# A Fourier mixer branch on one Trainium2 core: positions before channels, on sums and differences of token halves

## The chip, the cores and the metric

One core of one Trainium2 chip runs the whole program. The metric is device microseconds of one execution. All data is float32; matrix products run on pairs of numbers, a rounded high part (fp32r) and the remainder, called `hi` and `lo` below.

## The reference

An encoder layer for 512 tokens (SEQ) of 1024 features. The part that matters here is the mixer between the two feed-forward halves:

```
h = RMSNorm(x)
[q | k | v | f | g_a | g_b] = h @ w_in           # 512 | 128 | 128 | 512 | 1024 | 1024 columns
y_a = WindowGQA(q, k, v) @ w_branch_a
y_b = Re(FFT2 over (position, channel of a group)(f)) @ w_branch_b     # 4 groups of 128 channels
x = x + (sigmoid(g_a) * y_a + sigmoid(g_b) * y_b) @ w_out
```

With scale s = 1/sqrt(512*128), the Fourier branch of one group with the 512x128 matrix f is s*(C f c - S f d), where C and S are the 512x512 tables of cosines and sines over positions and c and d those of size 128 over channels.

## The kernel before

Every product `w*x` is three matmuls: w_hi with x_hi, w_hi with x_lo, w_lo with x_hi. One operand is loaded into the array (LDWEIGHTS, 128x128) and the other streams through it (up to 512 columns). A *granule* is one output tile of 128 features by 512 tokens: eight 128-row tiles of a weight matrix, each loaded in turn, while the tokens' columns stream, 24 matmuls of 512 columns. Weights come by DMA (issued by SP) into one of four slots of `raw`; ACT rounds a slot to `w_hi` (`split_hi`, L577), DVE subtracts to get `w_lo` (`split_lo`, L948), both four granules ahead, and both only when TensorE has used the slot's previous content (`w_used`).

All engines run fixed lists written out by hand, each engine in its own program order, tied by semaphores. In the mixer, one list (`MIXER`, L162) is read by ACT, DVE and TensorE (the loops at L819, L1238 and L1682); its first steps are

```
f 0; f 1; f 2; f 3; channels 0; k; v; positions 0; channels 1; q 0; positions 1; channels 2; q 1;
positions 2; channels 3; q 2; turn_v; positions 3; q 3; scores 0 0;
...
```

A step `f`, `k`, `v` or `q` is one granule on TensorE; then DVE reads the result out of PSUM and multiplies by the norm's factor of each token (`rstd`, made once during f 1 from sums of squares), ACT rounds it and DVE forms the remainder. In step `k` ACT writes four half-height tiles `kp_hi` and DVE four `kp_lo`. `channels g` multiplies, for each of the four blocks of 128 tokens, the block of f (loaded in the array) with the 256 columns of c and d: 12 matmuls of 256 columns, whose results, `ab`, have tokens on the partitions. ACT and DVE split them to `ab_hi` and `ab_lo`. `positions g` multiplies them with the position tables for outputs 0 to 257: two sums (even with C, odd with S) over four token blocks, 24 matmuls of 258 columns. ACT copies the even part to `even_t`; DVE adds and subtracts the odd part to obtain the 512 outputs in `y_t` (L1293, L1295), which ACT and DVE split to `fy_hi` and `fy_lo`. Each of these, and the two per-token sums at L1514 and L1524, waits for its inputs and for the PSUM bank that it overwrites to have been read.

Of the kernel before, what the change touches and what calls it, by code (L numbers as in the profile page):

```python
# [66 lines left out]
O_K = O_F + N_FGROUPS  # L67
# [9 lines left out]
B_SUM, B_RSTD = 4, 5  # L77
B_CH, B_POS = 4, 6
# [24 lines left out]
NPOS = SEQ // 2 + 2  # L103
CH_AT = TB * 2 * NPOS
TABLE = CH_AT + 2 * FG_DIM

# [23 lines left out]
def shape_constants():  # L130

    s, k = np.arange(SEQ)[:, None], np.arange(NPOS)[None, :]
    turn = 2 * np.pi * ((s * k) % SEQ) / SEQ
    scale = 1.0 / np.sqrt(SEQ * FG_DIM)
    pos = np.concatenate([np.cos(turn) * scale, -np.sin(turn) * scale], axis=1)
    pos = pos.reshape(TB, P, 2 * NPOS).transpose(1, 0, 2).reshape(P, CH_AT)
    c = np.arange(FG_DIM)
    turn = 2 * np.pi * ((c[:, None] * c[None, :]) % FG_DIM) / FG_DIM
    tables = np.concatenate([pos, np.cos(turn), np.sin(turn)], axis=1).astype(np.float32)
    onehot = np.zeros((N_BUCKETS, NREL + 1), np.float32)  # L140
    onehot[t5_buckets(), NREL - 1 - np.arange(NREL)] = 1.0
    return {"tables": tables, "onehot": onehot}


def window(nb):
# [17 lines left out]
    f 0; f 1; f 2; f 3; channels 0; k; v; positions 0; channels 1; q 0; positions 1; channels 2; q 1;  # L163
    positions 2; channels 3; q 2; turn_v; positions 3; q 3;
# [60 lines left out]
def build(nc, io):  # L225
# [10 lines left out]
    with ExitStack() as ctx:  # L236
# [13 lines left out]
        even_t, _, _ = place("even_t", [P, NPOS], F32)  # L250
# [39 lines left out]
        s_t = [s_a, s_b]  # L290
        y_t, _, _ = place("y_t", [P, SEQ], F32)
# [37 lines left out]
        ab_hi, ab_at = reuse("ab_hi", [P, TB, 2 * FG_DIM], F32R)  # L329
        ab_lo, _ = reuse("ab_lo", [P, TB, 2 * FG_DIM], F32R)  # L330
# [7 lines left out]
        tab_lo, _ = reuse("tab_lo", [P, TABLE], F32R)  # L338
        tab_raw, _, _ = place("tab_raw", [P, TABLE], F32, bias_at)

        pt_hi, pt_at, pt_size = place("pt_hi", [P, 2, GQ * BLK], F32R, ab_at)
        pt_lo, _, _ = place("pt_lo", [P, 2, GQ * BLK], F32R, ab_at + pt_size)
# [30 lines left out]
        pt_hi_ready, o_hi_ready, ab_hi_ready = sem("pt_hi_ready"), sem("o_hi_ready"), sem("ab_hi_ready")  # L373
        even_copied, y_hi_ready, m_hi_ready = sem("even_copied"), sem("y_hi_ready"), sem("m_hi_ready")
# [9 lines left out]
        pt_lo_ready, o_lo_ready, ab_lo_ready = sem("pt_lo_ready"), sem("o_lo_ready"), sem("ab_lo_ready")  # L384
# [9 lines left out]
        ab_done, even_done, odd_done, y_turned = sem("ab_done"), sem("even_done"), sem("odd_done"), sem("y_turned")  # L394
# [33 lines left out]
        def x_bank(m):  # L428

            return 8 - X_BANKS + m % X_BANKS  # L430

# [20 lines left out]
        def _(sp):  # L452
# [42 lines left out]
            for r in range(2):  # L495
# [77 lines left out]
        def _(act):  # L573
# [225 lines left out]
            for r in range(2):  # L799
# [19 lines left out]
                for step in steps:  # L819
                    kind = step[0]  # L820
                    if kind == "f":
                        grp = step[1]
                        split_hi(G_F + grp + SLOTS)
                        act.wait_ge(out_read, O_F + grp + 1)
                        copy(fy_hi[:, grp, :], gate_t[grp % 2][:, :]).then_inc(proj_hi_ready, 1)
# [24 lines left out]
                    elif kind == "turn_v":  # L850
                        act.wait_ge(v_turned, 1)
                        copy(v_hi[:, :, :], banks[B_CH][:, :]).then_inc(v_hi_ready, 1)
                    elif kind == "channels":
                        grp = step[1]
                        for i in range(2):
                            act.wait_ge(ab_done, 2 * grp + i + 1)
                            copy(ab_hi[:, 2 * i:2 * i + 2, :], banks[B_CH + i][:, :]).then_inc(ab_hi_ready, 1)
                    elif kind == "positions":
                        grp = step[1]
                        act.wait_ge(even_done, grp + 1)  # L860
                        if grp:
                            act.wait_ge(y_ready, 2 * grp)
                        copy(even_t[:, :], banks[B_POS][:, 0:NPOS]).then_inc(even_copied, 1)
                        act.wait_ge(y_ready, 2 * grp + 2)
                        copy(fy_hi[:, grp, :], y_t[:, :]).then_inc(y_hi_ready, 1)
# [79 lines left out]
        def _(dve):  # L945
# [35 lines left out]
            def factors(n):  # L981

                dve.wait_ge(rstd_done, n + 1)
                vec.tensor_copy(rstd[:, :], banks[B_RSTD][:, :]).then_inc(rstd_ready, 1)
                dve.wait_ge(rstd_ready, n + 1)

            def mean(n, blocks=(0, TB), nth=0):
                t0, t1 = blocks
                dve.wait_ge(sum_done, n + 1 + nth)
                vec.tensor_scalar(var[:, t0:t1], banks[B_SUM][:, 2 * t0:2 * t1:2], 1.0 / D_MODEL, EPS, ALU.mult,  # L990
# [233 lines left out]
            for r in range(2):  # L1224
# [13 lines left out]
                for step in steps:  # L1238
                    kind = step[0]
                    if kind == "f":  # L1240
                        grp = step[1]
                        split_lo(G_F + grp + SLOTS)
                        if grp == 0:
                            norm_factors(NORM_MIX)
                        dve.wait_ge(w_used, G_F + grp + 1)
                        vec.tensor_tensor(gate_t[grp % 2][:, :], banks[(O_F + grp) % BANKS][:, :], rstd[:, :],
                                          ALU.mult).then_inc(out_read, 1)
                        dve.wait_ge(proj_hi_ready, grp + 1)
                        lo(fy_lo[:, grp, :], gate_t[grp % 2][:, :], fy_hi[:, grp, :]).then_inc(proj_lo_ready, 1)
# [3 lines left out]
                    elif kind == "k":  # L1253
# [3 lines left out]
                        dve.wait_ge(proj_hi_ready, N_FGROUPS + 1)  # L1257
# [8 lines left out]
                    elif kind == "q":  # L1266
# [6 lines left out]
                        dve.wait_ge(proj_hi_ready, N_FGROUPS + 2 + c)  # L1273
# [3 lines left out]
                    elif kind == "turn_v":  # L1277
                        dve.wait_ge(v_hi_ready, 1)
                        lo(v_lo[:, :, :], banks[B_CH][:, :].rearrange("p (t d) -> p t d", t=TB),
                           v_hi[:, :, :]).then_inc(v_lo_ready, 1)  # L1280
                    elif kind == "channels":
                        grp = step[1]
                        for i in range(2):
                            dve.wait_ge(ab_hi_ready, 2 * grp + i + 1)
                            lo(ab_lo[:, 2 * i:2 * i + 2, :],
                               banks[B_CH + i][:, :].rearrange("p (t d) -> p t d", t=2),
                               ab_hi[:, 2 * i:2 * i + 2, :]).then_inc(ab_lo_ready, 1)
                    elif kind == "positions":

                        grp, h = step[1], SEQ // 2  # L1290
                        dve.wait_ge(odd_done, grp + 1)
                        dve.wait_ge(even_copied, grp + 1)
                        vec.tensor_tensor(y_t[:, 0:h + 1], even_t[:, 0:h + 1], banks[B_POS + 1][:, 0:h + 1],  # L1293
                                          ALU.add).then_inc(y_ready, 1)
                        vec.tensor_tensor(y_t[:, SEQ - 1:h:-1], even_t[:, 1:h], banks[B_POS + 1][:, 1:h],  # L1295
                                          ALU.subtract).then_inc(y_ready, 1)
                        dve.wait_ge(y_hi_ready, grp + 1)
                        lo(fy_lo[:, grp, :], y_t[:, :], fy_hi[:, grp, :]).then_inc(y_lo_ready, 1)
                    elif kind == "scores":
# [157 lines left out]
        def _(pe):  # L1457
# [56 lines left out]
            def sum_squares(n):  # L1514
# [4 lines left out]
                for t in range(TB):  # L1519
                    mm = nc.tensor.matmul(banks[B_SUM][:, 2 * t:2 * t + 2], ssum[:, t * P:(t + 1) * P], ones[:, 0:2],  # L1520
# [3 lines left out]
            def spread_factors(n):  # L1524

                pe.wait_ge(diag_ready, n + 1)
                nc.tensor.matmul(banks[B_RSTD][:, :], ones[:, :], gb_t[:, :], start=True, stop=True).then_inc(rstd_done, 1)
# [137 lines left out]
            for r in range(2):  # L1665
# [15 lines left out]

                for step in steps:  # L1682
# [199 lines left out]
```

## Time and profile before

| | us |
|---|---|
| median of 3 runs | 1013.51 (1012.17 to 1013.98) |
| the profiled execution | 1014.11 |
| its span in the trace | 1012.3 |
| TensorE matmuls busy in it | 997.7 |
| VectorE (DVE) busy | 679.0 |
| ScalarE (ACT) busy | 440.1 |

The span is the time from the first to the last recorded instruction; 1.8 us of the profiled execution lie outside it. Matmuls overlap, so the start of one to the start of the next tells more of their cost than the duration that the trace gives each. The mixer's first `f` matmul starts 365.87 us into the span and `channels 0` at 389.49 us; the first `scores` matmul starts at 439.87 us.

### The profile page before, as it was taken

Reading aid. Unit: us, or ns where it says so; the run is one execution under the profiler, and the core shown is the slowest. Engines: PE = TensorE matmul, PEld = TensorE weight load, DVE = VectorE, ACT = ScalarE, POOL = GpSimd, SP = SyncE. Lnnn points to the kernel's source line nnn. Section 1 sums busy time; section 2 is a strip of 40 time slices with the busy share of each in tenths; the row PEclk is TensorE's granted clock in tenths of the full one; section 3 lists DMA queues with packets and bytes.
Section 4 is the critical chain, followed back from the end, with each engine's and each line's share of the span. In section 5 each row is a group of like instructions: output and inputs, shape, how many; then the busy total and the mean of one; then the engine's idle time right before and its main releaser. Section 6 shows DMA issues by size and latency. Waiting matters only on the chain. (4 is left out here: it accounts for less than half of the span.)

```text
span 1012.3 us, 16276 instructions
## 1 busy us (share of the span) xinstructions
PE 997.7 (99%) x5872; PEld 885.7 (87%) x5872; DVE 679.0 (67%) x924; ACT 440.1 (43%) x656; POOL 198.1 (20%) x113
## 2 busy tenths in 40 slices
PE   8999999999999999999999999999999999999997
PEld 7789999999788888888888888888999999978887
DVE  5778999999534346667765555458899999943332
ACT  5344444446322325346664334334445454633322
POOL 2452333340011110000000001324234333001101
PEclk9999999999999999999999999999999999999999
DMA  6423334323433364212213343322333332333222
GB/s 210 132 66 94 116 92 120 87 83 96 124 96 90 115 171 125 63 42 62 63 42 89 98 124 104 104 84 72 96 108 100 110 97 83 89 117 96 88 68 84
DMA packets 191816, 98.81 MB, mean 98 GB/s; under 512 B 13384, under 2 KB 190616, under 8 KB 191648
## 3 DMA queue, kind: packets, MB, share of 16 engines
q1 hardware_dynamic: 190560, 95.50, 32.3%
q10 hardware_dynamic: 1216, 2.78, 0.8%
q8 instruction: 25, 0.41, 0.2%
q14 instruction: 15, 0.12, 0.0%
HBM read 96.15 MB, written 2.11 MB: 97 GB/s over the span
## 5 line engine op out<-in xcount | busy, mean ns | idle before, releaser
L575 ACT ACTIVATE w_hi<-raw 128x1024 fp32r<-128x1024 f32 (+2 forms) x202 | 181.5, 902 | 231.6 <-PE bank L1496 155.2
L953 DVE TENSOR_TENSOR w_lo<-raw,w_hi 128x1024 fp32r<-128x1024 f32 (+2 forms) x138 | 150.0, 1089 | 145.7 <-ACT w_hi L575 144.2
L1595 PE MATMUL bank<-t_lo,w_hi 128*128 128x256 f32 x896 | 224.7, 283 | 0.0
L1593 PE MATMUL bank<-t_hi,w_hi 128*128 128x256 f32 x896 | 224.6, 283 | 0.0
L1595 PEld LDWEIGHTS bank<-t_lo,w_hi 128*128 128x128 f32 x896 | 172.0, 192 | 0.2
L1593 PEld LDWEIGHTS bank<-t_hi,w_hi 128*128 128x128 f32 x896 | 172.0, 192 | 0.2
L1430 POOL TENSOR_TENSOR ssum<-ssum,sq 128x512 f32<-128x512 f32 x27 | 41.4, 1533 | 535.2 <-ACT sq L612 534.4
L1599 PE MATMUL bank<-t_hi,w_lo 128*128 128x256 f32 x896 | 144.0, 283 | 0.0
L1484 PE MATMUL bank<-a_hi,w_hi 128*128 128x512 f32 (+1 forms) x374 | 140.6, 380 | 1.7 <-ACT a_hi L575 1.7
L1485 PE MATMUL bank<-a_lo,w_hi 128*128 128x512 f32 (+1 forms) x374 | 139.4, 377 | 0.0
L1599 PEld LDWEIGHTS bank<-t_hi,w_lo 128*128 128x128 f32 x896 | 123.6, 192 | 0.0
L1121 DVE TENSOR_TENSOR w_lo<-raw,w_hi 128x1024 fp32r<-128x1024 f32 x64 | 90.9, 1420 | 9.3 <-ACT w_hi L575 9.3
L575 ACT ACTIVATE w_hi<-raw_b 128x1024 fp32r<-128x1024 f32 x64 | 60.8, 949 | 80.0 <-POOL raw_b L1450 40.4
L1121 DVE TENSOR_TENSOR w_lo<-raw_b,w_hi 128x1024 fp32r<-128x1024 f32 x64 | 92.8, 1449 | 3.8 <-ACT w_hi L575 3.7
L1496 PE MATMUL bank<-a_hi,w_lo 128*128 128x512 f32 (+1 forms) x374 | 91.1, 377 | 0.0
L1484 PEld LDWEIGHTS bank<-a_hi,w_hi 128*128 128x128 f32 x374 | 70.3, 188 | 15.4 <-ACT a_hi L575 2.5
L1484 PE MATMUL bank<-h_hi,w_hi 128*128 128x512 f32 x208 | 81.9, 394 | 0.3 <-DVE ga_t L1270 0.3
L1485 PEld LDWEIGHTS bank<-a_lo,w_hi 128*128 128x128 f32 x374 | 70.4, 188 | 12.6
L1485 PE MATMUL bank<-h_lo,w_hi 128*128 128x512 f32 x208 | 81.1, 390 | 0.0
L1496 PEld LDWEIGHTS bank<-a_hi,w_lo 128*128 128x128 f32 x374 | 67.8, 188 | 12.9
L1484 PE MATMUL bank<-hf_hi,w_hi 128*128 128x512 f32 x192 | 76.2, 397 | 0.0
L1485 PE MATMUL bank<-hf_lo,w_hi 128*128 128x512 f32 x192 | 75.7, 394 | 0.0
(230 smaller groups left out, 1494.6 us busy)
## 6 DMA issues: line engine op xcount, KB each, us to landing
raw<-in_w_down_dram SPq DMA_DIRECT2D x48, 384.0 KB, 3.0
raw_b<-in_w_up_dram SPq DMA_DIRECT2D x64, 256.0 KB, 3.7
raw<-in_w_up_dram SPq DMA_DIRECT2D x64, 256.0 KB, 3.6
raw<-in_w_up_dram SPq DMA_DIRECT2D x24, 512.0 KB, 3.9
raw<-in_w_in_dram SPq DMA_DIRECT2D x22, 512.0 KB, 3.7
raw<-in_w_down_dram SPq DMA_DIRECT2D x32, 128.0 KB, 2.2
raw<-in_w_out_dram SPq DMA_DIRECT2D x8, 512.0 KB, 3.4
x_rows<-in_x_dram SPq DMA_DIRECT2D x4, 512.0 KB, 7.8
```

The lines of the kernel that those rows point to most:

```text
L575: return nc.scalar.activation(dst, src, ACT.Copy, scale=scale)
L953: vec.tensor_tensor(w_lo[:, s, 0:nk, :], raw[:, s, 0:nk, :], w_hi[:, s, 0:nk, :].bitcast(F32), ALU.subtract).then_inc(w_lo_ready, 1)
L1121: vec.tensor_tensor(w_lo[:, slot, 0:nk, :], pair_raw[q % 2][:, slot, 0:nk, :], w_hi[:, slot, 0:nk, :].bitcast(F32), ALU.subtract).then_inc ...
L1430: nc.gpsimd.tensor_tensor(ssum[:, :], ssum[:, :], sq[:, m % 2, :], ALU.add).then_inc(sum_added, 1)
L1484: nc.tensor.matmul(out_ap, w_hi[:, s, k, :], xh, start=first and i == 0, stop=False)
L1485: mm = nc.tensor.matmul(out_ap, w_hi[:, s, k, :], xl, start=False, stop=False)
L1496: mm = nc.tensor.matmul(out_ap, w_lo[:, s, k, :], x_parts(k)[0], start=False, stop=last and i == len(tiles) - 1)
L1593: nc.tensor.matmul(out_ap, w_hi[:, slot, at_ + k, :], hi[:, k, :], start=first and k == 0, stop=False, skip_group_check=not first)
L1595: nc.tensor.matmul(out_ap, w_hi[:, slot, at_ + k, :], lo_[:, k, :], start=False, stop=False, skip_group_check=not first)
L1599: mm = nc.tensor.matmul(out_ap, w_lo[:, slot, at_ + k, :], hi[:, k, :], start=False, stop=k == HK - 1, skip_group_check=not first)
```

## The change

The two transforms are swapped. f is projected with tokens on the partitions: each `f j` step now holds two of the eight 128-row tiles of w_in with all 512 f columns (one DMA of two rows of 512 columns per partition in place of eight rows of 128), loads 128 tokens of h at a time and streams 512 weight columns, into four banks (4 to 7) that stay open over f 0 to f 3. That is again 24 matmuls of 512 columns for each step. During f 3, ACT scales the first two token blocks by `rinv` (the norm's factor, now one number for each partition), and DVE forms from them and the other two blocks two differences and two sums (`uv`), which ACT and DVE split. `positions g` multiplies u and v with tables of half the length, odd outputs from the differences and even ones from the sums: 12 matmuls of 256 columns, and the result is split once. `channels g` has the channel tables in the array: 3 matmuls of 256 columns for the sines (two blocks of 128 columns, apart by 256, read and written) and 3 of 258 for the cosines. ACT copies the cosines' part (258 columns) and two single edge columns; DVE writes `y_t` in four operations of 128 or 127 columns with every second column written.

The order of the steps and the loads (SP):

```diff
-    f 0; f 1; f 2; f 3; channels 0; k; v; positions 0; channels 1; q 0; positions 1; channels 2; q 1;
-    positions 2; channels 3; q 2; turn_v; positions 3; q 3;
+    f 0; f 1; f 2; f 3; k; positions 0; v; positions 1; channels 0; q 0; positions 2; channels 1; q 1; positions 3;
+    channels 2; q 2; turn_v; channels 3; q 3;
...
-                    g, col = G_F + c, Q_WIDTH + 2 * KV_WIDTH + c * FG_DIM
-                    load(g, raw[:, g % SLOTS, :, :], w_in[:, :, col:col + P])
+                    g, col = G_F + c, Q_WIDTH + 2 * KV_WIDTH
+                    load(g, raw[:, g % SLOTS, :, :].rearrange("p (k f) n -> p k (f n)", k=2),
+                         w_in[:, 2 * c:2 * c + 2, col:col + F_WIDTH])
```

ACT, in step `f`:

```diff
+                        if grp == N_FGROUPS - 1:
+                            act.wait_ge(rinv_ready, NORM_MIX + 1)
+                            for t in range(TP):
+                                act.wait_ge(f_done, t + 1)
+                                copy(gate_t[t][:, :], banks[B_F[t]][:, :], scale=rinv[:, t:t + 1]).then_inc(f_copied, 1)
+                            for nth, i in enumerate((0, 2, 1, 3)):
+                                act.wait_ge(uv_formed, nth + 1)
+                                copy(uv_hi[:, i, :], uv_of(i)).then_inc(uv_hi_ready, 1)
                         split_hi(G_F + grp + SLOTS)
-                        act.wait_ge(out_read, O_F + grp + 1)
-                        copy(fy_hi[:, grp, :], gate_t[grp % 2][:, :]).then_inc(proj_hi_ready, 1)
```

ACT, in step `channels`:

```diff
+                        act.wait_ge(ch_done, grp + 1)
+                        if grp:
+                            act.wait_ge(y_lo_ready, grp)
+                        copy(cos_t[:, :], banks[B_COS][:, 0:NHALF + 2]).then_inc(cos_copied, 1)
+                        act.wait_ge(cos_copied, grp + 1)
+                        copy(y_t[:, 0:NHALF + 1:NHALF], cos_t[:, P:2 * P + 1:P]).then_inc(edges_ready, 1)
+                        act.wait_ge(edges_ready, grp + 1)
+                        act.wait_ge(y_ready, 4 * grp + 4)
+                        copy(fy_hi[:, grp, :], y_t[:, :]).then_inc(y_hi_ready, 1)
```

DVE, in step `f`:

```diff
+                        if grp == N_FGROUPS - 1:
+                            for t in range(TP):
+                                if t == 0:
+                                    dve.wait_ge(f_done, 3)
+                                else:
+                                    dve.wait_ge(w_used, G_F + N_FGROUPS)
+                                dve.wait_ge(f_copied, t + 1)
+                                for i, op in ((t, ALU.subtract), (TP + t, ALU.add)):
+                                    vec.scalar_tensor_tensor(out=uv_of(i), in0=banks[B_F[TP + t]][:, :],
+                                                             scalar=rinv[:, TP + t:TP + t + 1], in1=gate_t[t][:, :],
+                                                             op0=ALU.mult, op1=op).then_inc(uv_formed, 1)
+                            for nth, i in enumerate((0, 2, 1, 3)):
+                                dve.wait_ge(uv_hi_ready, nth + 1)
+                                lo(uv_lo[:, i, :], uv_of(i), uv_hi[:, i, :]).then_inc(uv_lo_ready, 1)
                         split_lo(G_F + grp + SLOTS)
```

DVE, in step `channels`, after a wait for `cos_copied`:

```diff
+                        for sign, odd, even in ((ALU.add, slice(1, h, 2), slice(2, h, 2)),
+                                                (ALU.subtract, slice(SEQ - 1, h, -2), slice(SEQ - 2, h, -2))):
+                            vec.tensor_tensor(y_t[:, odd], cos_t[:, 0:P], sines[:, S_ODD], sign).then_inc(y_ready, 1)
+                            vec.tensor_tensor(y_t[:, even], cos_t[:, P + 1:2 * P], sines[:, S_EVEN],
+                                              sign).then_inc(y_ready, 1)
```

TensorE, a step `f j` (`f_done` counts, in f 3, the blocks whose last matmul is through):

```diff
+                    pe.wait_ge(w_hi_ready, g + 1)
+                    for kk in range(2):
+                        k = 2 * j + kk
+                        h_ready(NORM_MIX)(k)
+                        for t in range(TB):
+                            o_ap = banks[B_F[t]][:, :]
+                            nc.tensor.matmul(o_ap, rows_of(h_hi, k, t), group_of_four(w_hi, slot, kk), start=k == 0, stop=False)
+                            nc.tensor.matmul(o_ap, rows_of(h_lo, k, t), group_of_four(w_hi, slot, kk), start=False, stop=False)
+                    pe.wait_ge(w_lo_ready, g + 1)
+                    for t in range(TB):
+                        for kk in range(2):
+                            mm = nc.tensor.matmul(banks[B_F[t]][:, :], rows_of(h_hi, 2 * j + kk, t), group_of_four(w_lo, slot, kk),
+                                                  start=False, stop=j == N_FGROUPS - 1 and kk == 1)
```

TensorE's waits ahead of `positions` and `channels`:

```diff
+                        if grp == 0:
+                            pe.wait_ge(uv_lo_ready, 2 * TP)
                             pe.wait_ge(tab_lo_ready, 1)
+                        if grp >= 2:
+                            pe.wait_ge(eo_lo_ready, grp - 1)
...
+                        pe.wait_ge(eo_lo_ready, grp + 1)
+                        if grp:
+                            pe.wait_ge(y_ready, 4 * grp)
```

## Rows read from the trace of the kernel before

**Rows 1.** The page: span, TensorE's busy time, and its granted clock by slices.

```profile
span 1012.3 us, 16276 instructions
...
PE 997.7 (99%) x5872; PEld 885.7 (87%) x5872; DVE 679.0 (67%) x924; ACT 440.1 (43%) x656; POOL 198.1 (20%) x113
...
PEclk9999999999999999999999999999999999999999
```

**Rows 2.** Waits of engine PE over the span, longest in total: engine, line, releaser, us, times.

```profile
PE bank L1536 <- DMA x_rows<-in_x_dram: 3.2, 1, 3.2
```

**Rows 3.** Busy time of each engine by stretch: from, to, us, busy (count) of PE, PEld, DVE, ACT, POOL, clock, DMA.

```profile
389.40:443.00 53.60, 53.28 (x308) 46.91 (x307) 33.60 (x51) 24.46 (x39) 0.00 (x0) 1.00 0.28 85
443.00:600.00 157.00, 155.86 (x741) 129.34 (x740) 101.71 (x236) 82.07 (x159) 0.00 (x0) 1.00 0.26 77
```

**Rows 4.** Timeline of PE from f 3's end to the first scores: start us, us.

```profile
389.49 0.28 PE L1461 MATMUL bank<-tab_hi,fy_hi 128*128 128x256 f32 x1
...
390.90 0.40 PE L1484 MATMUL bank<-h_hi,w_hi 128*128 128x512 f32 x1
...
396.36 0.39 PE L1484 MATMUL bank<-h_hi,w_hi 128*128 128x512 f32 x1
...
401.80 0.28 PE L1461 MATMUL bank<-tab_hi,ab_hi 128*128 128x258 f32 x1
...
404.69 0.28 PE L1461 MATMUL bank<-tab_hi,fy_hi 128*128 128x256 f32 x1
...
439.87 0.28 PE L1748 MATMUL bank<-kp_hi,qo_hi 128*128 128x256 f32 x1
...
440.10 0.28 PE L1748 MATMUL bank<-kp_hi,qo_hi 128*128 128x256 f32 x1
...
440.81 0.50 PE L1484 MATMUL bank<-h_hi,w_hi 128*128 128x512 f32 x1 [0.32 <-DVE ga_t L1270]
```

**Rows 5.** Timeline of DVE around it, the same columns.

```profile
352.73 0.75 DVE L963 SCALAR_TENSOR_TENSOR h_lo<-xT,consts,h_hi 128x512 fp32r<-128x512 f32 x1 [0.93 <-ACT h_hi L575]
...
397.73 1.23 DVE L953 TENSOR_TENSOR w_lo<-raw,w_hi 128x1024 fp32r<-128x1024 f32 x1 [0.98 <-ACT w_hi L575]
398.88 0.68 DVE L1256 TENSOR_TENSOR ga_t<-bank,rstd 128x512 f32<-128x512 f32 x1
402.18 2.79 DVE L957 TENSOR_TENSOR kp_lo<-ga_t,kp_hi 64x512 fp32r<-64x512 f32 x4 [2.62 <-ACT kp_hi L575]
405.00 1.23 DVE L953 TENSOR_TENSOR w_lo<-raw,w_hi 128x1024 fp32r<-128x1024 f32 x1
...
415.60 0.42 DVE L1293 TENSOR_TENSOR y_t<-even_t,bank 128x257 f32<-128x257 f32 x1
415.94 0.41 DVE L1295 TENSOR_TENSOR y_t<-even_t,bank 128x255 f32<-128x255 f32 x1
...
440.07 0.69 DVE L1270 SCALAR_TENSOR_TENSOR ga_t<-bank,rstd 128x512 f32<-128x512 f32 x1 [2.56 <-PE bank L1496]
```

**Rows 6.** Timeline of ACT during the same k step.

```profile
396.64 1.06 ACT L575 ACTIVATE w_hi<-raw 128x1024 fp32r<-128x1024 f32 x1 [0.82 <-PE bank L1496]
...
400.24 1.91 ACT L575 ACTIVATE kp_hi<-ga_t 64x512 fp32r<-64x512 f32 x3
```

**Rows 7.** Groups of instructions by form, 378.1 to 440.5 us: count, busy us, mean ns.

```profile
L957 DVE TENSOR_TENSOR ab_lo<-bank,ab_hi 128x512 fp32r<-128x512 f32 x8 | 5.1, 682 | 0.0
...
L575 ACT ACTIVATE ab_hi<-bank 128x512 fp32r<-128x512 f32 x8 | 4.3, 588 | 0.0
...
L957 DVE TENSOR_TENSOR fy_lo<-y_t,fy_hi 128x512 fp32r<-128x512 f32 x4 | 2.8, 693 | 2.8 <-ACT fy_hi L575 2.8
...
L575 ACT ACTIVATE fy_hi<-y_t 128x512 fp32r<-128x512 f32 x4 | 2.5, 632 | 9.5 <-DVE y_t L1295 9.5
...
L575 ACT ACTIVATE even_t<-bank 128x258 f32<-128x258 f32 x4 | 1.5, 386 | 0.2 <-PE bank L1466 0.2
...
L1270 DVE SCALAR_TENSOR_TENSOR gb_t<-bank,rstd 128x512 f32<-128x512 f32 x2 | 1.4, 692 | 4.3 <-PE bank L1496 4.3
```

More of the change, by code:

```diff
@@ L66 @@
 O_F = O_DOWN[0] + DK
-O_K = O_F + N_FGROUPS
+O_K = O_F
 O_V, O_Q = O_K + 1, O_K + 2
@@ L430, in x_bank, with uv_of, group_of_four @@
             return 8 - X_BANKS + m % X_BANKS
+        def uv_of(i):
+            return uv_t[:, i, :] if i < 3 else ub_t[:, :]
+        def group_of_four(t, slot, kk):
+            return t[:, slot, N_FGROUPS * kk:N_FGROUPS * (kk + 1), :].rearrange("p f n -> p (f n)")
         def half_rows(v):
@@ L1282, in _ @@
                         grp = step[1]
[L1283 to L1296, printed above, removed]
+                        sines, h = banks[B_SIN], NHALF
+                        dve.wait_ge(cos_copied, grp + 1)
+                        for sign, odd, even in ((ALU.add, slice(1, h, 2), slice(2, h, 2)),
[3 more added lines that the diff above has]
+                                              sign).then_inc(y_ready, 1)
                         dve.wait_ge(y_hi_ready, grp + 1)
                         lo(fy_lo[:, grp, :], y_t[:, :], fy_hi[:, grp, :]).then_inc(y_lo_ready, 1)
+                    elif kind == "positions":
+                        grp = step[1]
+                        dve.wait_ge(eo_hi_ready, grp + 1)
+                        lo(fy_lo[:, grp, :], banks[B_POS[grp % 2]][:, :], fy_hi[:, grp, :]).then_inc(eo_lo_ready, 1)
                     elif kind == "scores":
@@ L1526, in spread_factors @@
                 pe.wait_ge(diag_ready, n + 1)
-                nc.tensor.matmul(banks[B_RSTD][:, :], ones[:, :], gb_t[:, :], start=True, stop=True).then_inc(rstd_done, 1)
+                nc.tensor.matmul(banks[B_RSTD[n]][:, :], ones[:, :], gb_t[:, :], start=True, stop=True).then_inc(rstd_done, 1)
             def x_tile(m):
@@ L1708, in _ @@
                         grp = step[1]
-                        pe.wait_ge(proj_lo_ready, grp + 1)
-                        if grp == 0:
-                            pe.wait_ge(tab_lo_ready, 1)
-                        else:
-                            pe.wait_ge(ab_lo_ready, 2 * grp)
-                        ch = slice(CH_AT, CH_AT + 2 * FG_DIM)
-                        for t in range(TB):
-                            tok = slice(t * P, (t + 1) * P)
-                            o_ap = banks[B_CH + t // 2][:, (t % 2) * 2 * FG_DIM:(t % 2 + 1) * 2 * FG_DIM]
-                            mm = passes(o_ap, [((fy_hi[:, grp, tok], fy_lo[:, grp, tok]),
-                                                (tab_hi[:, ch], tab_lo[:, ch]))])
-                            if t % 2:
-                                mm.then_inc(ab_done, 1)
+                        pe.wait_ge(eo_lo_ready, grp + 1)
@@ new lines, in _, with of_sines, of_cosines @@
+                        if grp:
+                            pe.wait_ge(y_ready, 4 * grp)
+                        def of_sines(t):
+                            return t.rearrange("p (b n) -> p b n", n=P)[:, 0:TB:TB - 1, :]
+                        def of_cosines(t):
+                            return t[:, C_ALL]
+                        for at_, part, o_ap in ((FG_DIM, of_sines, of_sines(banks[B_SIN][:, :])),
+                                                (0, of_cosines, banks[B_COS][:, 0:NHALF + 2])):
+                            ch = slice(CH_AT + at_, CH_AT + at_ + FG_DIM)
+                            mm = passes(o_ap, [((tab_hi[:, ch], tab_lo[:, ch]),
+                                                (part(fy_hi[:, grp, :]), part(fy_lo[:, grp, :])))])
@@ new lines, in _ @@
+                        if grp >= 2:
+                            pe.wait_ge(eo_lo_ready, grp - 1)
+                        ch = slice(grp * FG_DIM, (grp + 1) * FG_DIM)
+                        for even in range(2):
+                            pairs = []
+                            for i in range(TP * even, TP * (even + 1)):
+                                k0 = i * NHALF
+                                pairs.append(((uv_hi[:, i, ch], uv_lo[:, i, ch]),
+                                              (tab_hi[:, k0:k0 + NHALF], tab_lo[:, k0:k0 + NHALF])))
+                            mm = passes(banks[B_POS[grp % 2]][:, even * NHALF:(even + 1) * NHALF], pairs)
```

113 lines of the change are left out of this document (55 added, 58 removed).

## The prediction

> **What bounds the kernel now.** I read the page first: TensorE is busy 997.7 of 1012.3 us and its granted clock is at full speed (the 2.4 GHz level) in nearly every slice, while DVE has 67% and ACT 43% [rows 1]. Then TensorE's waits over the span: the longest in total is 3.2 us, for the first input at the very start [rows 2]. Then the stage that the change touches and the one behind it: TensorE is busy 53.28 of 53.60 us and 155.86 of 157.00 us, DVE 33.60 and 101.71, ACT 24.46 and 82.07 [rows 3]. So TensorE's stream of matmuls is the bound there and after it, and a matmul taken out of the Fourier steps shortens the span by its start-to-start time, as long as ACT and DVE keep ahead. What is behind the Fourier steps is the same list of steps, released by TensorE's own progress, so I expect it to shift as a whole. Last I read the three timelines of the stage, since there the waits of the new order must be placed by hand.
>
> **TensorE's work.** The f steps: 24 matmuls of 512 columns for each step before and after, 96 in all. A granule of 24 takes 390.90 to 396.36 = 5.46 us, 0.227 us from start to start [rows 4]. The roles are swapped (h loaded, weights streamed), both operands are fp32r of the same shapes as before, and I take the same time: 0. Bounds below: nothing makes it less, since 512 columns go through either way; above: no overlap at all, 0.39 us each as the rows give one matmul alone, 96 x 0.163 = 15.6 us more. I take the nearest row, the granule.
> A `channels` step of 12 matmuls of 256 columns takes 389.49 to 390.90 = 1.41 us, a `positions` step of 24 of 258 columns 401.80 to 404.69 = 2.89 us [rows 4]. Before, four of each: 17.2 us. After: `positions` is 12 of 256 columns, which is what a `channels` step is now, 1.41 us; `channels` is 3 of 256 and 3 of 258, half of that, 0.71 us. Four of each: 8.5 us. TensorE is rid of 8.7 us. `turn_v`, k, v, q and both per-token sums keep their matmuls.
>
> **The new input of `positions 0`.** f 3 ends at 389.49 us of the old span in the new kernel too, because nothing in front of it on TensorE changes; k follows at once and ends 5.46 us later, at 394.95. The release of another engine comes 0.28 us after the next granule starts (396.36 to 396.64, [rows 4, 6]); the third block's last matmul is two matmuls (0.45 us) before the end of f 3, so DVE starts on the differences at about 389.3. Four operations on 512 columns at 0.69 us [rows 7], or 0.75 as one with a scalar from memory took [rows 5], and four remainders at 0.69 [rows 7] end at 394.9 to 395.1; ACT's copies (0.59 to 0.63 each, [rows 7]) run beside them and lead. That is `uv_lo` just when TensorE arrives. The four scalings by `rstd` and the four remainders of f that DVE loses are as much as the eight that it gains, but now they come in one piece. Being late by up to about 1 us costs nothing there, for the reason in the next part. The tables are 1280 columns rather than 2320 and their rounding is early in either case, beside f 2: 0. The loads bring the same bytes in longer rows and lie beside the end of the feed-forward stage: 0; if they were late it would show as TensorE waiting for w_hi in f 0 to f 3, which the trace has nothing of now.
>
> **The wait that is added.** `channels 0` now waits for the remainder of `positions 0` (`eo_lo_ready`). On DVE this is queued behind all of step k. I read that step from before, with k's end at 396.36: ACT rounds a weight slot at 396.64, DVE subtracts it at 397.73 and evacuates k at 398.88, ACT writes four kp_hi until 402.15, DVE four kp_lo and is free at 405.00 [rows 5, 6]. So 8.64 us pass from k's end to the first moment at which DVE can take the remainder; it takes 0.69, and TensorE resumes 0.05 us after such a release (440.07 + 0.69 to 440.81, [rows 4, 5]): 9.4 us. TensorE has for this time positions 0, v and positions 1: 1.41 + 5.46 + 1.41 = 8.3 us. It waits 1.1 us. Before, this chain was hidden, since k, v and a Fourier step stood ahead of whatever needed it. The chain needs DVE free at 1.37 us behind k's end, 396.3; behind the remainders of uv stands one more weight subtraction of 1.23 us [rows 5], so it is free at 396.1 to 396.3. It just fits; whatever uv is later than that comes on top, one for one. Behind the waiting matmul only TensorE's own list is queued, and everything else waits for TensorE. Bounds of this wait: 0 (if DVE's steps overlap by more than the rows show) to 2 us (uv chain 0.9 late).
>
> **The steady part.** From q 0 to q 3 TensorE has 5.46 + 2.12 = 7.6 us for each round. For ACT and DVE, from the end of a q: 0.28, w_hi 1.06 and two halves of q at 0.64 each [rows 6] to 2.6; two remainders of q to 4.0; the remainder of `positions` to 4.7; four short additions; then ACT's fy_hi 0.63 and DVE's remainder 0.69 [rows 7]. No row shows the short additions (128 columns, every second column written). The pair of 257 and 255 columns starts 0.34 us apart and lasts 0.42 each [rows 5]; with 0.28 us for each further 257 columns (0.69 at 512, [rows 7]) one of 128 starts 0.20 after the other and lasts 0.28, four take 0.9. Ends: 0.5 (length alone) and 1.7 (as the whole 255 each). I take 0.9, and the round is through at 6.9 us, 0.7 ahead of TensorE; with 1.7 it is 0.1 late. In the round of q 2 the remainder of v (0.69) is added, and DVE is free just when q 3 ends. TensorE already waits 0.32 us there [rows 4]; up to 0.3 more, I take 0. In exchange ACT and DVE lose two halves of `ab` each round (2 x 0.59 and 2 x 0.68 [rows 7]).
>
> **The sum.** 8.7 - 1.1 = 7.6 us less. Against the profiled execution, 1014.1, that is 1006.5. The median of the runs is 0.6 below the profiled one, 1013.5, so for the median I say 1005.9.
>
> **A rule that speaks against it.** The sines' matmuls write two blocks of 128 columns that lie 256 apart in a PSUM bank and read such blocks; no row of before shows that. Bounds: the contiguous 0.12 us each, or, as two matmuls of 128 would be, twice that. I take 0.12, since each block is contiguous and long. The Trainium skill, "SBUF — State Buffer", section "Door 1: The DMA port swizzle", says that a PSUM access that isn't contiguous slows matmuls down significantly, as PSUM is accessed in units of two fp32 values; no run here shows it so far, and by it this is the rival C below.
>
> **The rivals.** 0.2% (2 us) is about what a measurement of this kernel can tell.
> A, the forecast, with 0.5 to 1.8 us of wait ahead of `channels 0`: 1005.2 to 1006.8. For it: the k chain is read off in the same order. Chance 0.60.
> B: no wait arises, the full 8.7 us: 1004.8. Against it: kp_hi and kp_lo alone are 5.3 us in line. 0.08.
> C: the 12 sines' matmuls take twice as long: 12 x 0.12 = 1.4 us more, 1007.3. 0.10.
> D: ACT and DVE become the bound of the rounds. From 0.4 us start to start of each short addition (0.2 and a fourth of 0.7) the round is longer than TensorE's; at 0.84, twice the 255-column row, 4 x 0.64 - 0.7 = 1.9 us in each of three rounds, 5.6 us, 1011.5. For it: writes to every second column, and more hand-overs between ACT and DVE than before. Against it: the backward write of L1295 costs no more than the forward one. With smaller amounts of the same kind, 1008 to 1011.5: 0.12.
> E, slower: the projection's matmuls no longer overlap, because an accumulation changes its bank at every second matmul and weights are streamed. It decides from 0.227 + 7.6/96 = 0.306 us start to start; at 0.39 it costs 15.6 us: 1013.5 - 7.6 + 15.6 = 1021.5. Against it: the `scores` matmuls at 439.87 and 440.10 are two pairs in different banks and start 0.12 apart from each other [rows 4]. 0.06.
> F: the change's matmuls are fewer, but a wait that I don't see takes most of it, 1011.5 to 1013.5: 0.04.
>
> **How the numbers follow.** The forecast is A's, 1005.9. The range 1004.3 to 1009.8 holds A, B, C and about half of D: 0.84. Faster by over 0.2%: A, B, C, D and some of F, 0.91; within 0.2%: 0.03; slower, E: 0.06.
>
> **What would show it.** In the trace after: 96 matmuls of f at 0.227 us start to start; `positions` 1.4 us and `channels` 0.7 us; one wait of TensorE of about 1.1 us ahead of `channels 0`, put down to DVE's fy_lo; none over 0.5 us ahead of `positions 0` or the later `channels`; the first `scores` at 432.3 us instead of 439.87; from there on the old distances. Wrong it would be if TensorE's busy time fell by much less than 8.7 us (C, E), or if it fell so and idle time took it (D, F).

## The result and the profile after

The changed kernel takes 1005.98 us (median of 4 runs, 1005.64 to 1006.02) against 1013.37 us (4 runs, 1012.17 to 1013.98): ratio 0.9927, 95% interval 0.9915 to 0.9939, 7.4 us less. In five more runs on another occasion it took 1005.48 us against 1012.93, ratio 0.9917 (0.9903 to 0.9931). The forecast was 1005.9.

The page of the kernel after (the same lines as [rows 1]):

```profile
span 1003.8 us, 16136 instructions
...
PE 988.9 (99%) x5800; PEld 876.6 (87%) x5800; DVE 676.0 (67%) x928; ACT 439.8 (44%) x658; POOL 197.8 (20%) x113
...
PEclk9999999999999999999999999999999999999999
```

The spans differ by 8.5 us, more than the medians. Three stretches of the two traces tell why. Up to the first f matmul: 365.87 us before and 364.67 after. That lies within the spread of executions: in the eleven traces of this document the first f matmul starts anywhere from 363.55 to 366.08 us, and TensorE's wait for the first input at the very start, 3.2 us in [rows 2] and 2.7 after, is part of it. From the first f matmul to the first `scores` matmul: 439.87 - 365.87 = 74.00 us before and 431.31 - 364.67 = 66.64 after, 7.36 less. From there to the end: 572.43 and 572.49, the same. So the gain is in the stretch that was changed, and what follows shifted as a whole. Below, "the stage" is that middle stretch and "the tail" the last. The stage is 66.64 or 66.65 us in five traces (the changed kernel's two, and the three versions below with additions in the `channels` steps, which hold nothing up before the tail); of the kernel before there is one trace. And the tail is 572.40 to 572.49 us in all eight in which nothing holds it up (spans are given to 0.1 us), while single runs of one kernel differ by 1 us and more. So the two are the finer measure.

Busy time from about the end of f 3 to a little behind the first `scores`, and from there on (the columns of [rows 3]). In the first row TensorE now idles 1.2 us (0.3 before), and DVE is at 72% (31.11 of 43.50), up from 63%; in the second the shares are those of before.

```profile
389.50:433.00 43.50, 42.29 (x223) 36.18 (x222) 31.11 (x54) 22.73 (x39) 0.00 (x0) 1.00 0.29 91
433.00:592.00 159.00, 157.87 (x749) 131.04 (x749) 103.11 (x238) 83.78 (x160) 0.00 (x0) 1.00 0.26 77
```

TensorE's waits over the span. One is new, 0.9 us on DVE's `fy_lo` (the operation that forms the remainder of `positions 0`):

```profile
PE bank L1571 <- DMA x_rows<-in_x_dram: 2.7, 2, 2.4
...
PE bank L1496 <- DVE fy_lo L986: 0.9, 1, 0.9
```

TensorE's timeline (start us, us), to be read against [rows 4]: the first f matmul at 364.67, the last eight matmuls of f 3 from 386.47, k from 388.29, `positions 0` from 393.73, v from 395.16, `positions 1` from 400.62, `channels 0` from 403.11 (sines) and 403.57 (cosines), q 0 from 403.93, `channels 1` from 410.82, the first scores at 431.31. The last line is the first gate granule behind them; the padding experiments below measure at that place.

```profile
364.67 0.39 PE L1731 MATMUL bank<-w_hi,h_hi 128*128 128x512 f32 x1
...
386.47 1.98 PE L1736 MATMUL bank<-w_lo,h_hi 128*128 128x512 f32 x8
388.29 0.39 PE L1519 MATMUL bank<-h_hi,w_hi 128*128 128x512 f32 x1
...
393.73 0.28 PE L1496 MATMUL bank<-tab_hi,uv_hi 128*128 128x256 f32 x1
...
395.16 0.40 PE L1519 MATMUL bank<-h_hi,w_hi 128*128 128x512 f32 x1
...
400.62 0.28 PE L1496 MATMUL bank<-tab_hi,uv_hi 128*128 128x256 f32 x1
...
403.11 0.39 PE L1496 MATMUL bank<-fy_hi,tab_hi 128*128 128x256 f32 x1 [0.89 <-DVE fy_lo L986]
403.33 0.28 PE L1497 MATMUL bank<-fy_lo,tab_hi 128*128 128x256 f32 x1
...
403.93 0.39 PE L1519 MATMUL bank<-h_hi,w_hi 128*128 128x512 f32 x1
...
410.82 0.28 PE L1496 MATMUL bank<-fy_hi,tab_hi 128*128 128x256 f32 x1
410.94 0.28 PE L1497 MATMUL bank<-fy_lo,tab_hi 128*128 128x256 f32 x1
...
411.55 0.40 PE L1519 MATMUL bank<-h_hi,w_hi 128*128 128x512 f32 x1
...
431.31 0.28 PE L1815 MATMUL bank<-kp_hi,qo_hi 128*128 128x256 f32 x1
...
432.25 0.50 PE L1519 MATMUL bank<-h_hi,w_hi 128*128 128x512 f32 x1 [0.31 <-DVE ga_t L1308]
```

DVE's timeline over the same stretch, to be read against [rows 5]: the first two of the operations that form uv, the four remainders, two weight subtractions, the four kp_lo, then the remainder of `positions 0` for which TensorE waits; two of the short additions; the end of the round of q 0 and the start of the next; the end of the round of q 2 and the evacuation of q 3.

```profile
388.03 1.41 DVE L1279 SCALAR_TENSOR_TENSOR uv_t<-bank,rinv,ga_t 128x512 f32<-128x512 f32 x2 [2.59 <-PE bank L1736]
...
390.68 1.89 DVE L986 TENSOR_TENSOR uv_lo<-uv_t,uv_hi 128x512 fp32r<-128x512 f32 x3
392.48 0.69 DVE L986 TENSOR_TENSOR uv_lo<-ub_t,uv_hi 128x512 fp32r<-128x512 f32 x1
393.08 1.22 DVE L982 TENSOR_TENSOR w_lo<-raw,w_hi 128x1024 fp32r<-128x1024 f32 x1
395.10 1.23 DVE L982 TENSOR_TENSOR w_lo<-raw,w_hi 128x1024 fp32r<-128x1024 f32 x1 [0.80 <-ACT w_hi L596]
...
399.55 2.78 DVE L986 TENSOR_TENSOR kp_lo<-ga_t,kp_hi 64x512 fp32r<-64x512 f32 x4 [2.62 <-ACT kp_hi L596]
402.36 0.69 DVE L986 TENSOR_TENSOR fy_lo<-bank,fy_hi 128x512 fp32r<-128x512 f32 x1
...
405.30 0.28 DVE L1325 TENSOR_TENSOR y_t<-cos_t,bank 128x128 f32<-128x128 f32 x1
405.50 0.28 DVE L1326 TENSOR_TENSOR y_t<-cos_t,bank 128x127 f32<-128x127 f32 x1
...
415.65 0.69 DVE L986 TENSOR_TENSOR fy_lo<-y_t,fy_hi 128x512 fp32r<-128x512 f32 x1 [0.76 <-ACT fy_hi L596]
417.24 0.69 DVE L1308 SCALAR_TENSOR_TENSOR ga_t<-bank,rstd 128x512 f32<-128x512 f32 x1 [0.89 <-PE bank L1531]
...
430.58 0.69 DVE L986 TENSOR_TENSOR fy_lo<-y_t,fy_hi 128x512 fp32r<-128x512 f32 x1 [0.76 <-ACT fy_hi L596]
431.50 0.69 DVE L1308 SCALAR_TENSOR_TENSOR ga_t<-bank,rstd 128x512 f32<-128x512 f32 x1 [0.23 <-PE bank L1531]
```

ACT's part of step k is the same as in [rows 6]: `w_hi` begins at 394.01, 0.28 us after k's end, and the last kp_hi ends at 399.51.

### The profile page after: what moved, and what is told of

Same layout as the page of the kernel before. It is cut to its first block and busy times, and to the rows that moved or that the text cites. A ratio compares the mean times of both kernels' runs of the same rounds, so it can differ in the third digit from the quotient of the medians.

```text
span 1003.8 us, 16136 instructions
## 1 busy us (share of the span) xinstructions
PE 988.9 (99%) x5800; PEld 876.6 (87%) x5800; DVE 676.0 (67%) x928; ACT 439.8 (44%) x658; POOL 197.8 (20%) x113
## 5 line engine op out<-in xcount | busy, mean ns | idle before, releaser
L1519 PE MATMUL bank<-h_hi,w_hi 128*128 128x512 f32 x176 | 69.0, 392 | 0.3 <-DVE ga_t L1308 0.3
L1520 PE MATMUL bank<-h_lo,w_hi 128*128 128x512 f32 x176 | 68.7, 390 | 0.0
```

What stands on the lines that cost most here:

```text
L1519: nc.tensor.matmul(out_ap, w_hi[:, s, k, :], xh, start=first and i == 0, stop=False)
L1520: mm = nc.tensor.matmul(out_ap, w_hi[:, s, k, :], xl, start=False, stop=False)
```

## The experiments

All are measured on the stage and the tail of one trace each. All but the last two were timed in turn with the kernel before: the changed kernel four times, pad_channels eleven times, the others five. The kernel before had a median of 1013.37 us on the occasion of the changed kernel's row, 1012.93 for the four rows behind it and 1012.63 for the next three; a ratio is to the one of its own occasion. The last two rows are single runs, whose times can't be compared: pad_channels1's is the longer although its tail is shorter, since its first f matmul came 1.8 us later.

| | median us | ratio to the kernel before (95%) | stage us | tail us |
|---|---|---|---|---|
| kernel before | 1013.37 | | 74.00 | 572.43 |
| changed kernel | 1005.98 | 0.9927 (0.9915 to 0.9939) | 66.64 | 572.49 |
| after_again | 1005.48 | 0.9917 (0.9903 to 0.9931) | 66.65 | 572.48 |
| positions0_first | 1004.37 | 0.9914 (0.9901 to 0.9928) | 65.52 | 572.43 |
| weights_between | 1004.86 | 0.9921 (0.9907 to 0.9934) | 66.79 | 572.40 |
| pad3 | 1006.00 | 0.9937 (0.9923 to 0.9950) | 67.84 | 572.49 |
| half_positions | 1006.42 | 0.9943 (0.9929 to 0.9956) | 68.26 | 572.42 |
| channels_twice | 1008.90 | 0.9966 (0.9952 to 0.9979) | 69.48 | 572.48 |
| pad_channels | 1010.26 | 0.9982 (0.9973 to 0.9991) | 66.64 | 577.01 |
| pad_channels2 | 1006.51 (one run) | | 66.65 | 573.78 |
| pad_channels1 | 1007.28 (one run) | | 66.65 | 572.77 |

**The changed kernel again.** No edit.

> The changed kernel unaltered, as the base for the others of this chip. It was 7.4 us below the kernel before in its median (1005.98 to 1013.37); 7.2 to 7.7 us again, with one wait of TensorE of about 0.9 us ahead of channels 0.

The median is 7.45 us below that of the kernel before, the stage is the same to 0.01 us, and the wait ahead of `channels 0` is 0.90 us.

**The wait is an order of DVE's list.** ACT and DVE walk the list with `positions 0` ahead of `k`; TensorE keeps its own:

```diff
+    early = [st for st in steps if st != ("positions", 0)]
+    early.insert(early.index(("k",)), ("positions", 0))
...
-                for step in steps:
+                for step in early:
```

> ACT and DVE take their part of positions 0 ahead of step k; TensorE's order is unchanged. Theory (the wait ahead of channels 0 is only DVE's queue order, the remainder of positions 0 standing behind four kp_lo): the wait is gone, DVE is done with the remainder about 3 us after k's end, and the span is 1.0 us shorter than the changed kernel's, 1004.9 us. Rival 1 (the k chain is only shifted by 3 us and stops TensorE later, at q 1 or channels 1): no gain, a new wait of about 1 us. Rival 2 (the wait is the time that a result needs to pass through ACT and DVE, whatever their order): the wait stays.

The stage is 1.12 us shorter than the changed kernel's, and TensorE has no wait ahead of `channels 0` or anywhere else from f 3 to the first `scores` (first line). DVE's timeline shows the order: the remainder of `positions 0` at 396.27 instead of behind the kp_lo, which now end at 404.46.

```profile
402.34 0.28 PE L1498 MATMUL bank<-fy_hi,tab_hi 128*128 128x256 f32 x1
```

```profile
396.27 0.69 DVE L988 TENSOR_TENSOR fy_lo<-bank,fy_hi 128x512 fp32r<-128x512 f32 x1 [1.69 <-ACT fy_hi L598]
...
401.67 2.79 DVE L988 TENSOR_TENSOR kp_lo<-ga_t,kp_hi 64x512 fp32r<-64x512 f32 x4 [2.62 <-ACT kp_hi L598]
```

Counted from k's end the kp_lo are 1.8 us later than in the changed kernel, and they stop nobody. Both rivals fall. The medians are 1.1 us apart too (1005.48 and 1004.37 us), but the intervals overlap, and the next version, whose stage is longer, has a median nearly as low (1004.86); it is the traces that settle it. By them this version is better than both kernels.

**Does a late uv cost anything?** DVE takes the weight subtraction of f 3 ahead of the last two uv remainders:

```diff
                             for nth, i in enumerate((0, 2, 1, 3)):
+                                if nth == 2:
+                                    split_lo(G_F + grp + SLOTS)
                                 dve.wait_ge(uv_hi_ready, nth + 1)
                                 lo(uv_lo[:, i, :], uv_of(i), uv_hi[:, i, :]).then_inc(uv_lo_ready, 1)
-                        split_lo(G_F + grp + SLOTS)
+                        else:
+                            split_lo(G_F + grp + SLOTS)
```

> In f 3, DVE does the weight subtraction that followed the four uv remainders ahead of the last two of them, so uv_lo is complete about 1.7 us later (394.9 rather than 393.2 on the changed kernel's span) but DVE is free no later than the k chain needs it (395.1). Theory (a late uv is absorbed by the wait ahead of channels 0, since that one is counted from k's end): TensorE waits about 1.2 us ahead of positions 0, the wait ahead of channels 0 falls from 0.9 to about 0, and the time is 0 to 0.3 us longer. Rival (the waits add up): 1.2 us longer, both waits present.

TensorE's timeline: a wait of 1.01 us ahead of `positions 0`, none ahead of `channels 0`. The stage grew by 0.15 us, not by the length of the wait. Two waits in line that are counted from the same event (k's end, here at 393.77) don't add up; the longer one decides: held up by uv, TensorE is at `channels 0` 9.60 us after k's end, where the remainder of `positions 0` let it go on after 9.38 us in the changed kernel.

```profile
394.94 0.39 PE L1499 MATMUL bank<-tab_hi,uv_hi 128*128 128x256 f32 x1 [1.01 <-DVE uv_lo L986]
...
403.37 0.28 PE L1499 MATMUL bank<-fy_hi,tab_hi 128*128 128x256 f32 x1
```

**Lateness beyond the slack.** Three additions ahead of the uv remainders (2.1 us of DVE):

```diff
+                            for n_pad in range(3):
+                                if n_pad:
+                                    dve.wait_ge(padded, n_pad)
+                                vec.tensor_tensor(y_t[:, :], rstd[:, :], rstd[:, :], ALU.add).then_inc(padded, 1)
                             for nth, i in enumerate((0, 2, 1, 3)):
```

> Three additions of 512 columns that nothing reads are put ahead of the four uv remainders on DVE, 0.7 us each, 2.1 us in all. Theory (lateness beyond DVE's slack before the k chain, 0.8 us in the changed kernel, comes on top one for one; up to it nothing is lost): TensorE waits 1.6 to 1.7 us ahead of positions 0 and 0.5 us ahead of channels 0, the time is 1.3 us longer than the changed kernel's. Rival (the waits add up): 1.6 us or more, both waits at full length. Second rival (DVE has slack enough everywhere): no change.

Waits of 1.39 and 0.40 us, and the stage 1.20 us longer: close to the theory's 1.3, not 1.6 or more. The additions took 2.05 us of DVE (389.89 to 391.94). It evacuates k 3.69 us after k's end (392.93), 1.18 us later than in the changed kernel (2.51); the other 0.87 us went into the time in which DVE had waited there (0.80 us at 395.10 above).

```profile
389.89 2.13 DVE L1286 TENSOR_TENSOR y_t<-rstd 128x512 f32<-128x512 f32 x3
391.94 1.89 DVE L987 TENSOR_TENSOR uv_lo<-uv_t,uv_hi 128x512 fp32r<-128x512 f32 x3
...
396.62 0.68 DVE L1299 TENSOR_TENSOR ga_t<-bank,rstd 128x512 f32<-128x512 f32 x1
```

```profile
394.48 0.39 PE L1501 MATMUL bank<-tab_hi,uv_hi 128*128 128x256 f32 x1 [1.39 <-DVE uv_lo L987]
...
403.48 0.39 PE L1501 MATMUL bank<-fy_hi,tab_hi 128*128 128x256 f32 x1 [0.40 <-DVE fy_lo L987]
```

**Half of the positions' matmuls alone.** In the kernel before, with the tokens of the last two blocks left out of each sum over positions:

```diff
                             pairs = []
-                            for t in range(TB):
+                            for t in range(TP):
```

> The kernel before, with positions summed over the first two of the four token blocks alone (the other half of each sum is left out): 12 matmuls of 258 columns in place of 24, nothing else changed. Theory (every matmul taken out of the Fourier steps shortens the time by its start-to-start distance, since TensorE is the bound there and all that follows shifts): 48 matmuls at 0.12 us, 5.8 us less from the first f matmul to the first scores (74.0 to 68.2 us), and about 1007.1 us. Rival (DVE, with about 65% in this stage, becomes the bound of the shorter rounds): less than 5 us, with waits of TensorE on DVE.

Stage 68.26 us, 5.74 less for 48 matmuls: 0.120 us each, the start-to-start time of [rows 4]. TensorE's list of waits has no new one; the only one on DVE's evacuations is the 0.3 us that [rows 4] show at 440.81:

```profile
PE bank L1485 <- DVE ga_t L1271: 0.3, 1, 0.3
```

**More matmuls in the new channels step.** In the changed kernel each pass is run twice, the second time over the first:

```diff
-                            mm = passes(o_ap, [((tab_hi[:, ch], tab_lo[:, ch]),
-                                                (part(fy_hi[:, grp, :]), part(fy_lo[:, grp, :])))])
+                            for _ in range(2):
+                                mm = passes(o_ap, [((tab_hi[:, ch], tab_lo[:, ch]),
+                                                    (part(fy_hi[:, grp, :]), part(fy_lo[:, grp, :])))])
```

> The changed kernel with the six matmuls of each channels step run twice (the second time over the first), 24 more matmuls of 256 and 258 columns. Theory: TensorE's stream is still the bound, 4 x 0.71 = 2.8 us more, 66.6 to 69.5 us from the first f matmul to the first scores, the sines' split columns at the same 0.12 us start to start. Rival (ACT and DVE pace the rounds in the new order, and TensorE has time over): less than 1.5 us more.

Stage 69.48 us, 2.84 more for 24 matmuls, 0.118 us each: TensorE is still the bound. In its timeline the sines' matmuls (from 410.63, columns in two blocks) and the cosines' (from 411.35) all start 0.12 us apart:

```profile
410.63 0.28 PE L1496 MATMUL bank<-fy_hi,tab_hi 128*128 128x256 f32 x1
410.75 0.28 PE L1497 MATMUL bank<-fy_lo,tab_hi 128*128 128x256 f32 x1
```

**How far DVE is from being the bound of the rounds.** Three additions at the end of each `channels` step:

```diff
                         lo(fy_lo[:, grp, :], y_t[:, :], fy_hi[:, grp, :]).then_inc(y_lo_ready, 1)
+                        for n_pad in range(3 * grp, 3 * grp + 3):
+                            if n_pad:
+                                dve.wait_ge(padded, n_pad)
+                            vec.tensor_tensor(uv_t[:, 0, :], rstd[:, :], rstd[:, :], ALU.add).then_inc(padded, 1)
```

> The changed kernel with three additions of 512 columns that nothing reads at the end of each channels step on DVE, 2.1 us for each group. Theory (a round of DVE has about 0.9 us to spare, a little more where it waits for ACT, and none of what it does is waited for by TensorE before the end of q 3): no new wait at the later channels and positions; DVE's lateness adds up over the rounds to about 3.2 us at the evacuation of q 3, and TensorE waits that long, on top of its 0.3 us, ahead of the first gate granule: 3.2 us more (2.5 to 3.7). Rival 1 (TensorE waits at each channels step, as it does ahead of channels 0): over 4 us, in several waits. Rival 2 (DVE has room, 64% busy before): under 1 us.

The place was right: the stage is unchanged and the whole loss begins with one wait ahead of the first gate granule, in the tail. The size was not: the wait is 3.81 us, 3.50 more than without the additions (3.2 expected), and the tail is 4.52 us longer, more than the 3.7 that I had as the most. TensorE's timeline shows what the other 1.0 us is: the matmuls of 512 columns start 0.23 us apart at first after the wait, then 0.43, and from 439.56 on 0.23 again. The busy time by stretch (the last columns are the granted clock, the DMA share and GB/s) has the clock at 1.00 throughout the wait, at 0.98 in the first microsecond of work, at 0.50 from 435.6 to 438.6 us and then at 0.86: it fell from the 2.4 GHz to the 1.2 GHz level about 1 us after work had resumed. The eight matmuls from 435.73 to 439.07 took 1.5 us more than at full clock; 0.5 us of that comes back at the next `scores` step, which in the changed kernel begins behind a wait on DVE (0.23 us idle) and here behind none.

```profile
434.62 0.50 PE L1524 MATMUL bank<-h_hi,w_hi 128*128 128x512 f32 x1 [3.81 <-DVE ga_t L1309]
434.96 0.40 PE L1525 MATMUL bank<-h_lo,w_hi 128*128 128x512 f32 x1
...
437.01 0.63 PE L1525 MATMUL bank<-h_lo,w_hi 128*128 128x512 f32 x1
437.44 0.63 PE L1524 MATMUL bank<-h_hi,w_hi 128*128 128x512 f32 x1
```

```profile
430.00:434.60 4.60, 0.82 (x6) 0.57 (x4) 3.77 (x9) 1.15 (x2) 0.00 (x0) 1.00 0.00 0
434.60:435.60 1.00, 0.98 (x4) 0.84 (x5) 0.57 (x1) 0.99 (x2) 0.00 (x0) 0.98 0.00 0
...
436.60:437.60 1.00, 1.00 (x4) 0.81 (x3) 0.96 (x2) 0.57 (x1) 0.00 (x0) 0.50 0.66 199
...
438.60:440.00 1.40, 1.40 (x8) 1.20 (x8) 0.48 (x3) 0.00 (x0) 0.00 (x0) 0.86 0.07 12
```

Two shorter versions separate the wait from the clock. With two additions:

> As pad_channels, with two additions for each group, 1.4 us. From its DVE timeline: DVE's lateness at the evacuation of q 3 is about 1.2 us, TensorE waits 1.5 us there. Theory (the 1.1 us beyond the wait in pad_channels came from the granted clock, which fell to half after 3.8 us without matmuls): after 1.5 us the clock stays at full, and the time to the end is 1.2 us longer than the changed kernel's, no more than the wait has grown. Rival (the rest of pad_channels' loss is a second effect of late ACT and DVE work, behind q 3): about a third more than the wait has grown, 1.5 us or more, at full clock.

A wait of 1.65 us (1.34 more), the tail 1.29 us longer, and the clock stays at 1.00:

```profile
433.19 0.50 PE L1524 MATMUL bank<-h_hi,w_hi 128*128 128x512 f32 x1 [1.65 <-DVE ga_t L1309]
```

```profile
434.00:440.00 6.00, 5.74 (x28) 4.55 (x27) 3.76 (x15) 3.46 (x9) 0.00 (x0) 1.00 0.16 48
```

With one addition:

> As pad_channels, with one addition for each group, 0.7 us. Theory (the slack of DVE in the last round is about 0.2 us, 0.9 in the others): TensorE waits 0.8 us ahead of the first gate granule in place of 0.3, 0.5 us more to the end. Rival (slack of 0.9 us everywhere): no change.

A wait of 0.59 us, 0.28 more, and 0.28 us on the tail, where 0.5 was expected. DVE's timeline has the two terms that I had wrong: the addition takes 0.60 us to the start of the next operation, not its full 0.7, and in the changed kernel DVE was ready for q 3's evacuation 0.31 us before it could begin (430.58 + 0.61 to 431.50), not 0.2; 0.60 - 0.31 = 0.29.

```profile
432.00 0.69 DVE L987 TENSOR_TENSOR fy_lo<-y_t,fy_hi 128x512 fp32r<-128x512 f32 x1 [0.76 <-ACT fy_hi L597]
432.61 0.68 DVE L1334 TENSOR_TENSOR uv_t<-rstd 128x512 f32<-128x512 f32 x1
433.21 0.68 DVE L1309 SCALAR_TENSOR_TENSOR ga_t<-bank,rstd 128x512 f32<-128x512 f32 x1
```

So up to 1.65 us the loss is the wait, and at 3.81 us the clock adds about 1.0 us. Between the two no length was tried.

## Why the prediction was right

**TensorE's work.** Forecast 8.7 us less. Measured: `positions` 393.73 to 395.16 = 1.43 us (forecast 1.41), `channels` 410.82 to 411.55 = 0.73 us (0.71), but 0.82 for the first, which starts after a wait, and 0.80 for the last, behind `turn_v`. The eight steps add up to 8.8 us against 17.3 before: 8.5 us less. The two experiments on matmul counts show that the exchange is one for one on both sides, -0.120 and +0.118 us a matmul. The projection kept its price, with four banks in turn and weights streamed: f 0 to f 3 take 23.62 us in both kernels (364.67 to 388.29, and 365.87 to 389.49), and f 3's last eight matmuls 1.82 us (386.47 to 388.29), 0.227 each. Rival E is refuted.

**The added wait.** Forecast 1.1 us ahead of `channels 0`, on DVE's `fy_lo`, from a chain of 9.4 us after k's end against 8.3 us of matmuls. Measured from k's end at 393.73: DVE takes the remainder at 402.36, 8.63 us later (forecast 8.64), TensorE resumes at 9.38 (9.4), and it would have gone on at 402.05, 8.32 (8.3): 1.06 us (the 0.89 that the trace gives count from the end of the matmul before, which overlaps the next one where nothing waits). positions0_first shows the cause, the order of DVE's list, by removing it. Rival B, no wait, is what that version achieves, not this one. (A wait of 0.5 to 1.8 us gives 1005.3 to 1006.6 by the forecast's own sum, not the 1005.2 to 1006.8 written under A; nothing else goes by these bounds.)

**The sum.** 8.5 - 1.06 = 7.4, and the stage is 7.36 us shorter; forecast 7.6. The tail kept its length (572.43 and 572.49 us), as assumed, and no wait that I had not named appeared (rival F). That the median came out within 0.1 us of 1005.9 is luck on top of a sound sum: the terms were 0.2 us off, and the interval of the ratio alone is 1.2 us to either side.

**The uv chain.** Here the working was too pessimistic by 0.5 to 0.7 us: it ended at 393.17, 0.56 us ahead of TensorE, where the forecast had it arriving at the same moment. The eight operations on DVE start 0.66 (with a scalar from memory) and 0.60 us apart, and I had added their full lengths (which, from 389.3, make 394.8 to 395.1 rather than 394.9). The claim that lateness there is free up to about 1 us is shown by weights_between (1.01 us of wait for 0.15 of time), and that what goes beyond DVE's slack counts in full by pad3 (1.18 us of lateness, 1.20 us of time).

**The rounds.** Four short additions: 0.20 us start to start and 0.28 long, exactly as taken, with every second column written. The round of q 0 ended on DVE at 416.34, 0.70 us before q 1 was through on TensorE at 417.04 (forecast 0.7). Rival D is refuted for this kernel.

For the round of q 2 I forecast the right thing, DVE free just when q 3 ends, from two misreadings that cancel. I had added the remainder of v to a full round of DVE and taken TensorE's full 7.6 us. But `positions 3` lies ahead of q 2: the remainder of v takes the place of that of a `positions` step, and the weight subtraction of this round has half the columns (0.69 us), so DVE was through at 431.27, 6.58 us after q 2's end (424.69). And TensorE has no `positions` step there either: it needs 6.62 us, to 431.31. That DVE's margin came out at about nothing was luck.

The padding runs say what it takes to make DVE late, and that my point for it was wrong: I had set it where the round gets longer than TensorE's, 0.7 us more, and one more operation of about that size already costs 0.28 us in all. TensorE met no new wait inside the rounds even with 2.1 us more in each. What decides is DVE's lateness at q 3's evacuation, and there it has only 0.31 us to spare.

**Rival C and the rule on PSUM.** The three sines' matmuls of `channels 1`, with two blocks of 128 columns read and written and 256 columns between the blocks, start 0.12 us apart from 410.82 on, as contiguous ones of 256 do; channels_twice has six of them at 0.12 us. (In `channels 0` the second starts 0.22 us after the first, at 403.33, but so does it with contiguous columns behind a wait: 0.22 us in pad3, 394.48 to 394.70.) The Trainium skill, "SBUF — State Buffer", section "Door 1: The DMA port swizzle", says that any PSUM pattern that isn't contiguous slows matmuls significantly. For two long blocks in one bank the measurement says no; a pattern of short pieces was not tried.

## What to carry to other kernels

Where one engine's stream is the bound and the rest is released by its progress, a removed instruction is worth its start-to-start time, and the correction to be made is for the results that the new order asks for earlier: read from the old trace how long the consuming engine's queue takes from the releasing event, and compare it with the work left in between. When a result is late only because it stands behind another step's work in an in-order queue, move it in that queue alone, and leave the bounding engine's order as it is. Waits counted from the same event overlap: shortening the first of two gains nothing while the second is longer.

## What the runs showed of the hardware

- After 3.81 us without matmuls (one trace, pad_channels) the granted clock fell to the 1.2 GHz level, not in the pause but about 1 us after work had resumed, and stayed there for some 3 us: 512-column matmuls started 0.43 us apart instead of 0.23, about 1.0 us lost in the end. After 1.65 us without matmuls (pad_channels2) it did not fall. The Trainium skill, "TensorE: Matmul & The Clock Gate", section "What's actually happening", describes the throttled state as the default that activity releases; the trace agrees in that the clock came back while TensorE was at work.
- DVE: additions of 128 columns with a stride of two on the output cost 0.20 us start to start, as much as the estimate for contiguous ones from the rows of before (0.34 us at 257 columns, less 0.14 us for the 129 columns fewer). Operations of 512 columns that wait for nothing start 0.60 us apart and last 0.69; with a scalar from memory, 0.66 and 0.74. An ACT copy of two columns takes 0.21 us.
